# Two blocks of layers on one core: the low part of each weight unit laid over its raw copy, and the feed-forward product kept in PSUM

## The reference

```python
for l in range(2):                                    # first block
    x = x + 0.5 * swiglu(rmsnorm(x), ...)             # D_FF = 2816
    h = rmsnorm(x); z = h @ w_in[l]                   # four branches and their gates
    g = sigmoid(z_gate)                               # 4 x 1024 columns
    merged = g0 * p_conf + g1 * p_sc + g2 * p_swa + g3 * p_fox
    x = x + merged @ w_out[l]
    x = x + 0.5 * swiglu(rmsnorm(x), ...)
for i in range(4):                                    # second block
    x = x + mixer_i(rmsnorm(x))                       # diff attention, hgrn2, sgu, diff attention
    x = x + cross_attention(rmsnorm(x), memory)
    x = x + swiglu(rmsnorm(x), ...)
# swiglu(h) = (silu(h @ w_gate) * (h @ w_up)) @ w_down
```

## Time and profile before

| | |
|---|---|
| median of 3 runs | 3428.96 us (3428.06 to 3429.78) |
| profiled execution | 3425.56 us, span 3423.8 us |
| TensorE (PE) busy | 3123.5 us, 91% |
| GpSimd (POOL) busy | 2157.7 us, 63% |
| VectorE (DVE) busy | 1734.8 us, 51% |
| ScalarE (ACT) busy | 1298.6 us, 38% |
| mean granted TensorE clock | 0.946 |

### The profile page before, as it was taken

How to read it: one execution, slowest core, us unless ns; L and a number is a source line. 1 busy time by engine, 2 the same in 40 slices (tenths; PEclk the granted TensorE clock), 3 DMA queues, 4 the chain that set the end, 5 groups by cost and what they waited for, 6 DMA issues and landing times.

```text
span 3423.8 us, 58583 instructions
## 1 busy us (share of the span) xinstructions
PE 3123.5 (91%) x24608; PEld 3034.1 (89%) x24608; DVE 1734.8 (51%) x1929; ACT 1298.6 (38%) x1331; POOL 2157.7 (63%) x464
## 2 busy tenths in 40 slices
PE   7995899999968999977999987999999999879998
PEld 6995889999967899966989987889999899769898
DVE  4638336627294357274357258526524373543572
ACT  4342334343324343332443352334343333324332
POOL 5873457878744468742848771448876488428485
PEclk9998889999988899987999999999999999879999
DMA  6542334545532245521525541235554355315252
GB/s 209 192 177 98 107 118 160 182 172 189 186 111 99 97 150 187 197 108 50 195 101 187 182 148 38 89 114 182 195 185 148 112 184 185 135 50 185 99 189 106
DMA packets 73396, 496.12 MB, mean 145 GB/s; under 512 B 8027, under 2 KB 12763, under 8 KB 14084
## 3 DMA queue, kind: packets, MB, share of 16 engines
q1 hardware_dynamic: 67768, 485.85, 39.7%
q10 hardware_dynamic: 5452, 7.62, 1.0%
HBM read 490.01 MB, written 3.41 MB: 144 GB/s over the span
## 4 chain that ended last, share of the span: by engine, by line
issue 54%; POOL 37%; PE 6%; DVE 1%; POOLq 0%; ACT 0%; DVEq 0%; ACTq 0%
POOL wl L365 37%; PE G L404 1%; PE G L406 1%; PE G L405 1%; PE S L405 1%; PE S L404 1%; PE S L406 1%; DVE hg L2044 0%; POOLq L369 0%; DVE logf L2028 0%; DVE hg L2031 0%; DVE logf L2034 0%; POOLq L364 0%; DVE logf L2038 0%; ACT wh L951 0%
## 5 line engine op out<-in xcount | busy, mean ns | idle before, releaser
L365 POOL TENSOR_TENSOR wl<-raw,wh 128x2048 fp32r<-128x2048 f32 x460 | 2157.5, 4708 | 1235.8 <-ACT wh L951 1220.5
L404 PE MATMUL G<-ah,wl 128*128 128x256 f32 x4368 | 1253.3, 287 | 60.2 <-DVE z L1491 24.7
L405 PE MATMUL G<-al,wh 128*128 128x256 f32 x4368 | 1246.5, 285 | 0.0
L406 PE MATMUL G<-ah,wh 128*128 128x256 f32 x4368 | 1245.7, 285 | 0.0
L951 ACT ACTIVATE wh<-raw 128x2048 fp32r<-128x2048 f32 x457 | 866.0, 1909 | 598.6 <-PE S L406 294.6
L404 PEld LDWEIGHTS G<-ah,wl 128*128 128x128 f32 x4368 | 849.8, 195 | 71.5 <-issue 25.1
L405 PEld LDWEIGHTS G<-al,wh 128*128 128x128 f32 x4368 | 850.0, 195 | 0.2
L406 PEld LDWEIGHTS G<-ah,wh 128*128 128x128 f32 x4368 | 849.0, 194 | 0.0
L405 PE MATMUL S<-gl,wh 128*128 (+1 forms) x1408 | 398.5, 283 | 0.0
L406 PE MATMUL S<-gh,wh 128*128 (+1 forms) x1408 | 397.8, 282 | 0.0
L404 PE MATMUL S<-gh,wl 128*128 (+1 forms) x1408 | 394.6, 280 | 0.0
(11 more groups left out here) (325 smaller groups left out, 4459.6 us busy)
## 6 DMA issues: line engine op xcount, KB each, us to landing
raw<-w_units SPq DMA_DIRECT2D x460, 1024.0 KB, 4.8
bias<-tables ACTq DMA_DIRECT2D x24, 128.0 KB, 4.2
tables<-trow ACTq DMA_DIRECT2D x1, 1536.0 KB
x<-x_in SPq DMA_DIRECT2D x4, 256.0 KB, 5.1
con<-consts SPq DMA_DIRECT2D x1, 1024.0 KB, 15.2
memx<-mem_in ACTq DMA_DIRECT2D x1, 1024.0 KB, 5.0
out<-full SPq DMA_DIRECT2D x4, 256.0 KB, 2.5
tables<-trow ACTq DMA_DIRECT2D x1, 768.0 KB
```

The source lines that it names most:

```text
L365: pool.tensor_tensor(wl[:, j * UW:(j + 1) * UW], raw[:, j * UW:(j + 1) * UW], wh[:, j * UW:(j + 1) * UW].bitcast(F32), ALU.subtract)\
L404: pe.matmul(out, sl, vh, start=start and k == 0, stop=False, **kw)
L405: pe.matmul(out, sh, vl, start=False, stop=False, **kw)
L406: ins = pe.matmul(out, sh, vh, start=False, stop=stop and k == len(parts) - 1, **kw)
```

## The change

Two parts that have nothing in common but VectorE and GpSimd.

1. `wl` takes the same bytes as `raw`: GpSimd writes the difference over its input. A slot of `raw` is then read by TensorE, as `wl`, until the unit is done, so SyncE's DMA for unit n+4 waits for `unit_done` of unit n in place of `low_ready`. 32 KB in each partition are freed and stay unused. The number of DMAs, copies and subtractions is the same, and so is their order on each engine.
2. In `pair` the product of silu and value is written over the value in its PSUM bank, not to `full` in SBUF, and is cut from there. The bank is free for TensorE when `gl` is written (`gated_ready`), and no longer when the product is there (`gated`). `input_root` keeps its running value in the PSUM bank of the sums, not in `root`, and multiplies twice by the reciprocal in place of squaring it; it still has five operations.

```diff
     raw = sb("raw", RING * UW)
+    wl = sb("wl", RING * UW, F32R, offset=at[0] - 4 * RING * UW)
     wh = sb("wh", RING * UW, F32R)
-    wl = sb("wl", RING * UW, F32R)
...
-                    sp.wait_ge(low_ready, RING * i + (j + 1 - RING))
+                    sp.wait_ge(unit_done, RING * i + (j + 1 - RING))
                     sp.dma_start(raw[:, j * UW:(j + 1) * UW], w_units[i * RING + j, :, :])\
...
-                        free = (silu_ready, s0 + u // 2 - 1) if u % 2 == 0 else (gated, v0 + u // 2 - 1)
+                        free = (silu_ready, s0 + u // 2 - 1) if u % 2 == 0 else (gated_ready, v0 + u // 2 - 1)
...
             def input_root():
-                t, half, bank = root[:, 0:n], root[:, n:2 * n], s_next()[:, 0:n]
+                bank = s_next()[:, 0:n]
-                dve.tensor_scalar(half, bank, -0.5 / D, -0.5 * EPS, ALU.mult, ALU.add)\
+                dve.tensor_scalar(bank, bank, -0.5 / D, -0.5 * EPS, ALU.mult, ALU.add)\
                 dve.reciprocal(rr, rr).then_inc(vec_step, c.one(vec_step))
-                dve.tensor_tensor(t, rr, rr, ALU.mult).then_inc(vec_step, c.one(vec_step))
-                dve.tensor_tensor(t, t, half, ALU.mult).then_inc(vec_step, c.one(vec_step))
-                dve.scalar_tensor_tensor(rr, t, 1.5, rr, ALU.add, ALU.mult).then_inc(vec_step, c.one(vec_step))
+                for _ in range(2):
+                    dve.tensor_tensor(bank, bank, rr, ALU.mult).then_inc(vec_step, c.one(vec_step))
+                dve.scalar_tensor_tensor(rr, bank, 1.5, rr, ALU.add, ALU.mult)\
...
-                    if u // 2 >= 2:
-                        dve.wait_ge(gated_ready, p + (r0 - 1))
-                    dve.tensor_tensor(hf, sg, value, ALU.mult).then_inc(gated, 1)
+                    dve.tensor_tensor(value, sg, value, ALU.mult).then_inc(gated, 1)
-                    dve.tensor_copy(to_h, hf).then_inc(gated_high, 1)
+                    dve.tensor_copy(to_h, value).then_inc(gated_high, 1)
-                    dve.tensor_tensor(to_l, hf, to_h.bitcast(F32), ALU.subtract).then_inc(gated_ready, 1)
+                    dve.tensor_tensor(to_l, value, to_h.bitcast(F32), ALU.subtract).then_inc(gated_ready, 1)
```

More of the change, by code:

```diff
@@ L509, in ffn @@
                 n0 = unit[0]
-                s0, v0 = expect.get("silu_ready", 0), expect.get("gated", 0)
+                s0, v0 = expect.get("silu_ready", 0), c.taken.get("gated_ready", 0)
                 g0 = gbank[0]
@@ L536, in ffn @@
                         free = ((silu_ready, 2 * i + (s0 + u // 2 - 1)) if u % 2 == 0
-                                else (gated, 2 * i + (v0 + u // 2 - 1)))
+                                else (gated_ready, 2 * i + (v0 + u // 2 - 1)))
                         unit_of(u, u, RING * i + (n0 + u), free)
@@ L540, in ffn @@
                 gbank[0] += 2 * FP
-                expect["silu_ready"], expect["gated"] = s0 + FP, v0 + FP
+                expect["silu_ready"] = s0 + FP
                 for k in range(4):
@@ L544, in ffn @@
                     gfree[gbank[0] - 4 + k] = ((silu_ready, s0 + u // 2 + 1) if u % 2 == 0
-                                               else (gated, v0 + u // 2 + 1))
+                                               else (gated_ready, v0 + u // 2 + 1))
                 n1 = unit[0]
@@ L1446, in input_root @@
                 n = T + TB
-                t, half, bank = root[:, 0:n], root[:, n:2 * n], s_next()[:, 0:n]
+                bank = s_next()[:, 0:n]
                 dve.wait_ge(root_ready, c.next(root_ready))
-                dve.tensor_scalar(half, bank, -0.5 / D, -0.5 * EPS, ALU.mult, ALU.add)\
-                    .then_inc(mean_used, c.one(mean_used))
-                dve.reciprocal(rr, rr).then_inc(vec_step, c.one(vec_step))
-                dve.wait_ge(vec_step, c.sofar(vec_step))
-                dve.tensor_tensor(t, rr, rr, ALU.mult).then_inc(vec_step, c.one(vec_step))
-                dve.wait_ge(vec_step, c.sofar(vec_step))
-                dve.tensor_tensor(t, t, half, ALU.mult).then_inc(vec_step, c.one(vec_step))
-                dve.wait_ge(vec_step, c.sofar(vec_step))
-                dve.scalar_tensor_tensor(rr, t, 1.5, rr, ALU.add, ALU.mult).then_inc(vec_step, c.one(vec_step))
-                dve.wait_ge(vec_step, c.sofar(vec_step))
+                dve.tensor_scalar(bank, bank, -0.5 / D, -0.5 * EPS, ALU.mult, ALU.add)\
+                    .then_inc(vec_step, c.one(vec_step))
+                dve.reciprocal(rr, rr).then_inc(vec_step, c.one(vec_step))
+                for _ in range(2):
+                    dve.wait_ge(vec_step, c.sofar(vec_step))
+                    dve.tensor_tensor(bank, bank, rr, ALU.mult).then_inc(vec_step, c.one(vec_step))
+                dve.wait_ge(vec_step, c.sofar(vec_step))
+                dve.scalar_tensor_tensor(rr, bank, 1.5, rr, ALU.add, ALU.mult)\
+                    .then_inc(mean_used, c.one(mean_used))
+                dve.wait_ge(mean_used, c.sofar(mean_used))
             def pairs(ap):
@@ L1530, in pair @@
                     s = (u // 2) % 2
-                    sg, hf = full[:, s * 512:(s + 1) * 512], full[:, D + s * 512:D + (s + 1) * 512]
+                    sg = full[:, s * 512:(s + 1) * 512]
                     gate, value = G[(g0 + u - 1) % 4][:, :], G[(g0 + u) % 4][:, :]
```

## The result

The changed kernel takes **3461.22 us** (median of 4 runs, 3455.52 to 3465.21), the one before 3428.68 beside it: ratio 1.0095, 95% interval 1.0082 to 1.0107. The forecast was 3440 in 3419 to 3456: the sign was right, the time lies above the range. One of the twelve executions of the first kernel of experiment 5 took 8617.57 us, nothing on record says why, and it is left out of that kernel's ratio.

What follows compares the result with a forecast made beforehand. TensorE, busy 91% of the span, bounds the kernel, waiting mostly for VectorE and ScalarE. Terms +14.2 (`mix1`), -4.1 (`diff`), +0.9 (small) sum to +11.0 us on 3428.96: 3440 us, range 3419 to 3456.

Steps and rivals of the forecast that it cites:

- The supply: Weight path, steady state: subtraction ends at E + 11.6, weights wanted at E + 17.3, 5.7 us to spare, no cost.
- The rival that TensorE waits for weights at every unit: Landings behind unit ends take 11 us, every unit late by 0.5 us or more, 3500 and above; chance 0.08.
- The start: Kernel's start: table writes hold landings up, a transfer issued 8 us later waits behind them; 0 to +2, taken as 0.
- My own condition: Weight supply: if a landing took over 10 us, the cover of 5.7 us to spare would be gone.
- The gates: `mix1` run ends: late subtraction holds VectorE's product, 3.7, 2.7 and 3.7 us, 10.1 in each of two `mix1`.
- the gap of 1.1 us: `mix1` gates: `L1837` just fits before the next subtraction; four more products missing it, at 4.6 us each, give 3458.
- The root: `mix1` input root with PSUM input: one held-up operation freed, bounds 1.7 and 4.15, 3.0 us gained in each `mix1`.
- silu, product and cuts: Feed-forward: 88 casts to `gh` and 88 `gl` lose hold-ups, TensorE doesn't wait for them, so this gives nothing.
- The root and `diff`: Two `diff`: freed root operations gain 6.5 us in the first, 7.7 in the second; with costs, net -4.1.
- The price of the late subtraction: `diff`: softmax between groups 4 x 1.65 = 6.6 us later, `L1875` at the second's start 3.5; 10.1 in all.
- The casts: Feed-forward casts from PSUM take +0.26 us each, hidden beside matmuls; uncovered, 88 x 0.26 = 23 us.
- the signs named for right and wrong: Profile after: right if `wl` waits stay near 15 us and `L1834` averages near 4; wrong if `wl` leads or `L1834` stays 1.

Runs made afterwards that it cites:

- experiment 5: First kernel: changed kernel, gate's copy behind the sigmoid, held back behind a run's last gate, 3432.23 us; plus later second table write 3419.83; old kernel, PSUM root, later write 3392.87.
- experiment 3: Changed kernel with own `wl` and early wait (`low_ready`) up to unit 31: 3454.56 us; changed kernel with second table write sent in first `mix1`: 3451.05.
- Experiment 1: Kernel before, its transfers waiting for `unit_done` in place of `low_ready`, VectorE's code old: 3472.25 us; the same with `wl` laid over `raw`: 3469.42.
- experiment 2: Kernel before with only the input root's small products in PSUM: 3401.54 us; with all of VectorE's PSUM edits, early wait and own `wl`: 3405.65.

## Why the prediction was off

By the profiles the loss is 37.3 us, against the sum of 11. The 26.3 us between them are the start (12.0), the seven other `ffn` (11.7), the two `mix1` (11.4), the small stages (1.7), less what `diff` does better (10.5).

- **The supply: right.** "TensorE is fed with 5.7 us to spare": in steady state the low part is ready 11.6 us behind the unit's end, as forecast, and in the seven later feed-forward stages TensorE has no wait for weights from unit to unit. The rival that TensorE waits for weights at every unit is out.
- **The start: the step that failed first.** "A transfer issued 8 us later waits behind the same writes", 0 taken, at most 2; it was 12, and experiment 3 shows that the early wait takes it away. Units 7, 8 and 12 take 1.9, 5.1 and 4.3 us longer. I looked at the transfers that already met the writes and left out those that now would, units 6 and 7. My own condition stood paragraphs above, "If a landing took over 10 us, this cover would be gone", and the kernel before has landings of 15.1 us in the median there (its DMA issues from 30 to 110 us):

```profile
raw<-w_units SPq DMA_DIRECT2D x11, 1024.0 KB, 15.1
```

- **The gates: mechanism right, size wrong.** Forecast +20.2 in all, measured 29.6 at the run ends. The first two runs cost 4.0 and 3.2 in the first `mix1`, 3.7 and 2.9 in the second (forecast 3.7 and 2.7). The last run cost 6.2 and 9.6, forecast 3.7: the wait grew by the 3.7, and 2.5 came from TensorE's clock behind it; in the second `mix1` three sums missed the gap of 1.1 us, which was in the range's upper end and not in the sum, and the wait grew by 7.2. The clock isn't in the prediction at all. The root gave 3.9 us in the two `mix1` where 6.0 was forecast.
- **The seven other `ffn` and the starts: the second step that failed.** The sum has no term for them (of silu, product and cuts it says "this gives nothing", of stage starts nothing at all), measured +11.7. I followed the casts and the supply, and these cost nothing. I didn't ask where in a stage's start an operation of two SBUF inputs stands that TensorE waits for: `al`, 8.4 us at the first units behind six of these stages.
- **The root and `diff`: right in sign, gain too small, price too large, and credited to the wrong edit in part.** At the unit that waits for the root the two `diff` gained 9.3 and 7.8 us, forecast 6.5 and 7.7. The price of the late subtraction behind it was 2.5 us, forecast 10.1 (6.6 between the groups, 3.5 for `L1875`). Experiment 1 adds what I hadn't seen: the late subtraction itself gets out of the way of most of the root, 9.3 and 5.8 us without PSUM.
- **The casts: right.** 0.69 us each, beside matmuls, no time either way in the seven later `ffn`; in experiment 1 the 64 of one form were held to a mean of 4.3 us (`wl` in its own place), and these stages cost 12.2 us against 11.7.
- Of the signs named for right and wrong: `gl`, `gh`, the root, the landings and `qf` came as written, `L1832` has 3.2 us where I named 4, since six of the 24 meet no subtraction, and `wl` went to 24.1 us instead of staying near 15: nearly all of the growth is in the first 130 us (18.2 against 9.4).

What stays open: single `diff`, `cross` and `sgu` stages differ by 1 to 4 us between kernels with the same code there, and the 4.1 us between the two kernels of experiment 2 are of this kind. Where TensorE's clock rises and falls may be the cause; no run takes that apart. The `al` hold-ups (8.4 of the 11.7 us of the `ffn`) were read from the trace and not tested by a run, and the 3.2 us in the last units of the `ffn` have no cause that I could name.

## What to carry to other kernels

When a change makes GpSimd work later, list every VectorE operation with two SBUF inputs, and every cast from SBUF to SBUF, for which TensorE waits, stage starts included, and set each against GpSimd's new interval; the price is paid at the ends of runs, not inside them. Moving one operand into PSUM frees the operation, but the next one inherits the wait if it stands within the same subtraction; moving the subtraction frees the whole run, if the moved step isn't put ahead of something more urgent. The mean duration of the freed operation doesn't tell: it was 998 ns in a kernel that was 17 us slower than the one it should mend. A ring that is refilled later needs its slack checked where landings are slowest, not in steady state.

## What the runs showed of the hardware

- Issuing a DMA of 1536 KB to DRAM from ScalarE right behind another of 768 KB took 9.6 us of ScalarE's time (9.7 in the kernel before), where the same transfer by itself took 0.75.
- A VectorE product of two SBUF inputs that started inside a GpSimd subtraction ended 0.55 to 0.56 us behind its end, in all 18 cases; with one input in PSUM it took 0.70 us in the same place. A cast from SBUF to SBUF took 426 to 4885 ns in the kernel before, one from PSUM 0.69 everywhere.
- Behind a wait of 5.7 us TensorE's granted clock was 0.65 over the next 8.3 us (1.2 GHz in part), behind one of 2.1 us it was 1.00. The lost clock was two thirds as much again as the growth of the wait, 2.5 on 3.7 us, in the one place read closely.
- GpSimd's subtraction written over its own operand took 4654 ns, into a place of its own 4650, in two kernels that differ in nothing else: writing in place cost nothing.
